# Eight projection tiles of the first block as three products of rounded parts, and the last parameter rows turned earlier

## What is computed

```python
h = rms_norm(x, mix_norm_g[l])
proj = h @ w_in                               # 256 x 1024 by 1024 x (1664 + 512)
qa, ka, va, pb, qm = split_cols(proj, ...)    # attention q, k, v; ten tiles for the recurrence; memory q
pb = token_shift(pb, rwkv_mu[l])              # p + mu * (previous token's p - p)
r, k, v, wd, ad, gd = split_cols(pb, ...)
w = -softplus(-(w0 + tanh(wd) @ w2)) - 0.5    # three low-rank products: w2, a2, g2
a = sigmoid(a0 + ad @ a2)
g = sigmoid(gd) @ g2
kk = k * k_k; kk = kk / norm(kk); k = k * (1 + (a - 1) * k_a)
y = rwkv7_scan(r, w, k, v, -kk, kk * a)       # a recurrence over the tokens
mkv = rms_norm(mem, mem_norm_g) @ w_mem_kv    # keys and values of 256 memory tokens
x = x + concat([out_a, out_b, out_m]) @ w_out
```

## Time and profile before

| | |
|---|---|
| median of 3 runs | 1076.56 us (1076.35 to 1080.98) |
| the profiled execution's own time | 1078.08 us |
| its span, first to last instruction | 1076.3 us |
| PE busy | 915.3 us, 85% of the span |
| DVE busy | 540.1 us, 50% |
| ACT busy | 347.4 us, 32% |
| POOL busy | 76.2 us, 7% |
| mean granted TensorE clock | 0.941 of full |
| read from HBM | 312.24 MB, 291 GB/s over the span |

### The profile page before, as it was taken

How to read it: one execution, slowest core, us unless ns; L and a number is a source line. 1 busy time by engine, 2 the same in 40 slices (tenths; PEclk the granted TensorE clock), 3 DMA queues, 4 the chain that set the end, 5 groups by cost and what they waited for, 6 DMA issues and landing times.

```text
span 1076.3 us, 19223 instructions
## 1 busy us (share of the span) xinstructions
PE 915.3 (85%) x8378; PEld 703.6 (65%) x8378; DVE 540.1 (50%) x1008; ACT 347.4 (32%) x684; POOL 76.2 (7%) x113
## 2 busy tenths in 40 slices
PE   9999999999999999999999997766666666657665
PEld 8587788489999888988989954433333333334432
DVE  2476588858888767888767642211112111212121
ACT  4411355246776526455553331000001000000001
POOL 3101810000000000330010000000000000000000
PEclk9999999999999999999999999988889787889888
DMA  9344463685454664975446999999999999999994
GB/s 347 108 172 170 147 236 101 223 287 173 157 185 160 221 233 162 289 244 189 160 150 253 428 382 421 429 427 430 429 429 427 429 427 431 428 429 431 426 430 173
DMA packets 76106, 316.71 MB, mean 294 GB/s; under 512 B 3999, under 2 KB 27840, under 8 KB 63472
## 3 DMA queue, kind: packets, MB, share of 16 engines
q1 hardware_dynamic: 71252, 302.24, 71.3%
q0 software_dynamic: 4624, 13.14, 4.0%
q10 hardware_dynamic: 140, 0.04, 0.0%
HBM read 312.24 MB, written 1.06 MB: 291 GB/s over the span
## 4 chain that ended last, share of the span: by engine, by line
PE 59%; DMA 27%; DVE 8%; ACT 4%; issue 2%; ACTq 0%; SPq 0%; POOL 0%; DVEq 0%
PE ps L461 57%; DMA w<-in_w_up 19%; DMA w<-in_w_gate 6%; DMA w<-in_w_down 2%; DVE sp L1860 1%; DMA rot<-q 1%; PE ps L587 0%; PE ps L2702 0%; DVE acc L923 0%; ACT sp L1851 0%; ACT hts L2809 0%; ACT sd L2183 0%; PE ps L2115 0%; ACTq L3041 0%; DVE w L961 0%
## 5 line engine op out<-in xcount | busy, mean ns | idle before, releaser
L461 PE MATMUL ps<-w,xg 128*32 128x256 f32 x2048 | 158.9, 474 | 107.4 <-DMA w<-in_w_up 83.8
L461 PE MATMUL ps<-hb,sp 128*128 128x256 f32 x1824 | 224.5, 283 | 0.0
L461 PEld LDWEIGHTS ps<-hb,sp 128*128 128x128 f32 x1824 | 218.6, 188 | 3.9 <-issue 3.0
L461 PEld LDWEIGHTS ps<-w,xg 128*32 128x32 f32 x2048 | 84.4, 132 | 180.3 <-issue 156.3
L1860 DVE TENSOR_TENSOR sp<-w,sp 128x1024 fp32r<-128x1024 f32 x122 | 144.4, 1220 | 37.1 <-ACT sp L1851 37.1
L1851 ACT ACTIVATE sp<-w 128x1024 fp32r<-128x1024 f32 x122 | 122.1, 1051 | 42.1 <-PE ps L461 40.5
L2876 DVE TENSOR_TENSOR cst<-ps,cst 64x256 f32<-64x256 f32 x31 | 13.3, 428 | 224.0 <-ACT cst L2796 224.0
L2796 ACT ACTIVATE cst<-ps 64x256 f32<-64x256 f32 x31 | 11.7, 377 | 324.9 <-PE ps L461 324.9
L2902 DVE TENSOR_TENSOR ost<-ps,cst 32x256 f32<-32x256 f32 x120 | 50.5, 420 | 100.2 <-PE ps L461 97.4
L461 PE MATMUL ps<-w,hts 128*32 128x256 f32 x1024 | 62.1, 382 | 13.2 <-ACT hts L2809 11.4
L461 PE MATMUL ps<-sp,ab 128*128 128x512 f32 x264 | 61.7, 395 | 0.0
(11 more groups left out here) (415 smaller groups left out, 1164.4 us busy)
## 6 DMA issues: line engine op xcount, KB each, us to landing
w<-in_w_down SPq DMA_DIRECT2D x36, 2048.0 KB, 35.1
w<-in_w_gate SPq DMA_DIRECT2D x32, 2048.0 KB, 28.6
w<-in_w_up SPq DMA_DIRECT2D x32, 2048.0 KB, 32.4
w<-in_w_in SPq DMA_DIRECT2D x13, 2048.0 KB, 9.6
w<-in_w_up SPq DMA_DIRECT2D x22, 1024.0 KB, 7.7
w<-in_w_ada SPq DMA_DIRECT2D x8, 2048.0 KB, 8.5
w<-in_w_out SPq DMA_DIRECT2D x4, 2048.0 KB, 9.0
w<-in_w_ada POOLq DMA_DIRECT2D x8, 768.0 KB, 5.3
```

The costliest lines, as they stand in the source:

```text
L461: return q.eng.matmul(o, l, r, start=start, stop=stop, skip_group_check=True)
```

## The change

Eight of the tiles (9, 4, 5, 6, both tiles of the memory queries, 0 and 1) are done by `split_pe` in three float32r products for each k; tiles 8, 3, 2 and 7 and all others stay float32. For them ACT makes the high part of the input in four pieces (`h_hi_sc`) and of each tile's weights (`w_hi_sc`), DVE the low parts (`h_lo_ve`, `w_lo_ve`); the weights' low parts are written over the weights in their slot. `split_pe` waits until a tile's low part is there. The new buffers lie where other things lay, so some of those have moved (`va`, `vm`, `kb`) and two of POOL's DMAs wait: the spread bias for the memory queries, the gate biases for the fourth pair. The last two turns of parameter rows now stand after the first group of low-rank products, the bias product after the second. DVE and ACT do their work in another order. Two semaphores are merged with others, and the counts of the parts go up by 12; nothing else changes.

```diff
--- before.py
+++ after.py
...
@@ -186,9 +186,9 @@
         swb = sb("swb", P1 + 3216, 1536)
         swr = sb("swr", P1 + 4752, 1536)
         qk = sb("qk", P1 + 6288, 2048)
-        va = sb("va", P1 + 8336, 256)
-        vm = sb("vm", P1 + 8592, 512)
-        kb = sb("kb", P1 + 9104, 256)
+        va = sb("va", P1 + 9104, 256)
+        vm = sb("vm", P1 + 8336, 512)
+        kb = sb("kb", P1 + 8848, 256)
         cat = sb("cat", 41264, 2048)
         P_ = [sb(f"pr{i}", o, 512) for i, o in enumerate((44592, 45216, 45728))]
         PT_ = [sb(f"pt{i}", 46240 + 512 * i, 512) for i in range(2)]
@@ -209,6 +209,9 @@
         rs = sb("rs", 44592, 512)
         hT1 = sb("ht1", 45216, 2048)
         mT = sb("mt", 47264, 2048)
+        hT_hi, hT_lo = sb("hth", 27808, 2048, R), sb("htl", P1 + 6800, 2048, R)
+        slotr = [sb(f"wr{i}", 4096 * i, 4096, R) for i in range(3)]
+        w_hi = [sb(f"wh{i}", o, 1024, R) for i, o in enumerate((P1 + 3216, P1 + 4240, P1 + 5264, 41264, 49312, 43568))]
         rqs, rqt, nsink, vmu, yss = (RK[:, o:o + n] for o, n in ((0, 20), (20, 20), (40, 6), (48, 12), (64, 24)))
 
         pz = sb("pz", RB, 2570)
...
@@ -621,6 +625,58 @@
         def proj_pe(q, o, w, c0, act_v, ks=range(8)):
             for k in ks:
                 t = mm(q, o, w[:, k, c0:c0 + 128], act_v[:, k, :], k == 0, k == 7)
+            return t
+
+        SPLIT = [9, 4, 5, 6, ("q", 0), ("q", 1), 0, 1]
+        W_HI = {9: 0, 4: 1, 5: 3, 6: 2, ("q", 0): 1, ("q", 1): 5, 0: 4, 1: 0}
+        HI_AT = {w: 5 + n for n, w in enumerate(SPLIT)}
+
+        def w_of(w):
+            if w in R_AT:
+                c, c0 = R_AT[w]
+                return chunks["in", c], c0
+            return chunks["in", 0], 256 + 128 * w[1]
+
+        def whole(ch, c0, r=False):
+            return (slotr if r else slot)[ch.slot_no].rearrange("p (k n) -> p k n", k=8)[:, :, c0:c0 + 128]
+
+        def w_hi_sc(q, w):
+            ch, c0 = w_of(w)
+            q.wait_ge(*ch.tok)
+            if w in (9, ("q", 0), ("q", 1)):
+                q.wait_ge(s["in_a"], 16)
+            if w == ("q", 0):
+                q.wait_ge(s["rp"], 2)
+            if w == 1:
+                q.wait_ge(s["rp"], 1)
+            if w == 0:
+                q.wait_ge(s["nsc"], 6)
+            q.eng.activation(v(w_hi[W_HI[w]], 8), whole(ch, c0), ACT.Copy).then_inc(s["nhi"], 1)
+
+        def w_lo_ve(q, w):
+            ch, c0 = w_of(w)
+            q.wait_ge(s["nhi"], HI_AT[w])
+            q.eng.tensor_tensor(whole(ch, c0, True), whole(ch, c0), v(w_hi[W_HI[w]], 8).bitcast(F), SUB).then_inc(s["nlo"], 1)
+
+        def piece(a, i):
+            return v(a, 8)[:, 4 * (i % 2):4 * (i % 2) + 4, 128 * (i // 2):128 * (i // 2) + 128]
+
+        def h_hi_sc(q):
+            for i in range(4):
+                q.wait_ge(s["ht1"], i + 1)
+                q.eng.activation(piece(hT_hi, i), piece(hT1, i), ACT.Copy).then_inc(s["nhi"], 1)
+
+        def h_lo_ve(q):
+            for i in range(4):
+                q.wait_ge(s["nhi"], i + 1)
+                q.eng.tensor_tensor(piece(hT_lo, i), piece(hT1, i), piece(hT_hi, i).bitcast(F), SUB).then_inc(s["nlo"], 1)
+
+        def split_pe(q, o, w, ks):
+            ch, c0 = w_of(w)
+            q.wait_ge(s["nlo"], HI_AT[w])
+            hi, lo = v(w_hi[W_HI[w]], 8), whole(ch, c0, True)
+            for k in ks:
+                t = mm3(q, o, [hi[:, k, :], lo[:, k, :]], [v(p, 8)[:, k, :] for p in (hT_hi, hT_lo)], k == 0, k == 7)
             return t
 
         def rpair_steps(q, n):
@@ -631,7 +687,8 @@
                 ch = chunks["in", c]
                 q.wait_ge(*ch.tok)
                 for k in range(0, 8, 2):
-                    t = proj_pe(q, psum[b][:, 256 * h:256 * h + 256], cols8(ch, 128 if c == 4 else 512), c0, hv, (k, k + 1))
+                    o = psum[b][:, 256 * h:256 * h + 256]
+                    t = split_pe(q, o, tile, (k, k + 1)) if tile in SPLIT else proj_pe(q, o, cols8(ch, 128 if c == 4 else 512), c0, hv, (k, k + 1))
                     if h == 1 and k == 6:
                         t.then_inc(s["rp"], 1)
                         free[b] = [(s["rp_sb"], n + 1)]
@@ -640,11 +697,11 @@
         def first_pair_pe(q):
             take(q, 0)
             w = cols8(chunks["in", 0], 512)
-            for h, tile in enumerate(PAIRS[0]):
-                for z in range(2):
-                    q.wait_ge(*((s["in_a"], 16), chunks["in", 0].tok)[z])
-                    q.wait_ge(s["ht1"], 3 + z)
-                    t = proj_pe(q, psum[0][:, 256 * h:256 * h + 256], w, R_AT[tile][1], hv, range(4 * z, 4 * z + 4))
+            for z in range(2):
+                q.wait_ge(*((s["in_a"], 16), chunks["in", 0].tok)[z])
+                q.wait_ge(s["ht1"], 3 + z)
+                proj_pe(q, psum[0][:, 0:256], w, R_AT[8][1], hv, range(4 * z, 4 * z + 4))
+            t = split_pe(q, psum[0][:, 256:512], 9, range(8))
             t.then_inc(s["rp"], 1)
             free[0] = [(s["rp_sb"], 1)]
 
@@ -689,7 +746,8 @@
             w = cols8(chunks[name], 512)
             for z in range(4):
                 h = z // 2
-                t = proj_pe(q, psum[b][:, 256 * h:256 * h + 256], w, c0 + 128 * h, mv_ if n == 3 else hv, range(4 * (z % 2), 4 * (z % 2) + 4))
+                o, ks = psum[b][:, 256 * h:256 * h + 256], range(4 * (z % 2), 4 * (z % 2) + 4)
+                t = split_pe(q, o, ("q", h), ks) if n == 0 else proj_pe(q, o, w, c0 + 128 * h, mv_ if n == 3 else hv, ks)
                 if z == 3:
                     t.then_inc(s["qp"], 1)
                     free[b] = [(s["qk_sb"], 3 * n + 3)]
@@ -771,6 +829,7 @@
             q.wait_ge(s["bias_v"], 1)
             e.dma_start(scratch.ap(), Eb[0:6, :]).then_inc(s["bias"], 16)
             q.wait_ge(s["bias"], 16)
+            q.wait_ge(s["qp"], 1)
             e.dma_start(v(swr, 6), bass.AP(scratch, 0, [[1, 128], [384, 6], [1, 256]])).then_inc(s["bias"], 16)
 
         BANDB = (7, 1, 7)
...
@@ -3043,15 +3102,24 @@
             e.activation(sml(111, 1), cpad[:, 0:1], ACT.Sqrt)
             norms_sc(q, 0, x, (s["x_io"], 16), junk1)
             roots_sc(q, 0)
+            h_hi_sc(q)
+            w_hi_sc(q, 9)
             rpair_sc(q, 0)
+            w_hi_sc(q, 4)
+            w_hi_sc(q, 5)
             cpad_sc(q)
             lt_sc(q)
             norms_sc(q, 1, v(Xm, 2), (s["mem"], 16), junk1)
             rpair_sc(q, 1)
+            w_hi_sc(q, 6)
             lora_sc(q, 0)
+            w_hi_sc(q, ("q", 0))
             lora_sc(q, 1)
             rpair_sc(q, 2)
+            w_hi_sc(q, ("q", 1))
             lora_sc(q, 2)
+            w_hi_sc(q, 0)
+            w_hi_sc(q, 1)
             exp_sc(q)
             lam_sc(q)
             qpair_sc(q, 0)
@@ -3110,18 +3178,27 @@
             scaled_ve(q, 0, x, Xn)
             q.wait_ge(s["par_v"], 1)
             feat_ve(q, 0, hT1, col("mix_norm_g", 0, 8), "ht1")
+            h_lo_ve(q)
+            w_lo_ve(q, 9)
             par_ve(q, 1, 7)
             shift_ve(q, 0)
+            w_lo_ve(q, 4)
+            w_lo_ve(q, 5)
             norms_ve(q, 1)
             shift_ve(q, 1)
+            w_lo_ve(q, 6)
             scan_ve(q)
-            lam1_ve(q)
+            w_lo_ve(q, ("q", 0))
             par_ve(q, 2, 5)
             par_ve(q, 3, 6)
+            shift_ve(q, 2)
+            w_lo_ve(q, ("q", 1))
+            lam1_ve(q)
+            kksq_ve(q)
+            w_lo_ve(q, 0)
             bias_ve(q)
-            shift_ve(q, 2)
-            kksq_ve(q)
             kp_ve(q)
+            w_lo_ve(q, 1)
             hsum_ve(q, 0, HSB, rs, 1.0, 0.0, floor=1e-24)
             scaled_ve(q, 1, v(Xm, 2), Xm)
             feat_ve(q, 1, mT, col("mem_norm_g", 0, 8), "ht1")
@@ -3192,6 +3269,7 @@
             for d, src in plist2:
                 e.dma_start(d, src).then_inc(s["par2"], 16)
             bias_gp(q)
+            q.wait_ge(s["rp"], 4)
             e.dma_start(gb[0], bc(A["b_ada_2"][:, 2048:3072], [128, 1024])).then_inc(s["gb"], 16)
             for j in range(4):
                 e.dma_start(gq[32 * j:32 * j + 32, :], bc(A["b_ada_2"][:, 5120 + 256 * j:5376 + 256 * j], [32, 256])).then_inc(s["gb"], 16)
@@ -3239,11 +3317,13 @@
             for z in range(3):
                 for _ in lora_pe(q, z):
                     next(dense, END)
-            q.wait_ge(s["par2"], N_PAR2)
-            par_pe(q, 2, 5)
-            par_pe(q, 3, 6)
-            q.wait_ge(s["cst2"], 32)
-            bias_pe(q)
+                if z == 0:
+                    q.wait_ge(s["par2"], N_PAR2)
+                    par_pe(q, 2, 5)
+                    par_pe(q, 3, 6)
+                if z == 1:
+                    q.wait_ge(s["cst2"], 32)
+                    bias_pe(q)
             for _ in dense:
                 pass
             hsum_pe(q, 0, HSB, [bsv[:, i, :] for i in range(3)], "hs", (s["r_kk"], 2))
...
```

(5 more changed lines are left out.)

16 lines of the change are left out of this document (8 added, 8 removed).

## The result

The changed kernel takes **1083.06 us** (median of 21 executions, 1077.50 to 1095.61); the kernel before, run beside it, 1080.38 (21 executions, 1076.35 to 1083.83). The ratio is **1.0029, 95% interval 1.0016 to 1.0042**: 2.7 us slower by the medians, less than the 0.5% that the prediction took as what a measurement can tell, but more than this one is uncertain. The ratio is not the quotient of the two medians (1.0025): it is formed from the fast executions alone, without that of 1095.61, which shows a slower state. Forecast were 1076.0, in 1072.8 to 1079.0, and 0.6 us *less* than before. Of the 7.1 us between 1076.0 and 1083.06, 3.8 lie in the starting point: the forecast began from a median of three executions, 1076.56, and 21 have their median at 1080.38. The other 3.3 are the sign: 2.7 more in place of 0.6 less.

What follows compares the result with a forecast made beforehand. PE's work and holes were taken to bound the first 80 us, early gains or losses lasting to the end. Saved 9.5 less paid 8.9 leaves 0.6 us: 1076.56 - 0.6 = 1076.0, range 1072.8 to 1079.0.

Steps and rivals of the forecast that it cites:

- What PE saves: PE's split tiles: three float32r products take 0.351 us against 0.437 for one float32; 64 products save 5.5 us.
- Tile 9: After tile 8, PE waits 0.75 us for tile 9's low part, ready at 16.95 us.
- Tile 6: After three low-rank products, PE waits 0.9 us for tile 6's low part, ready at 32.4 us.
- The turned rows: At 34.9 us PE wants bank 5 and waits 1.4 us for DVE's copy of the first turn.
- The hole at the sums: After the queries, at 48.1 us, PE waits 0.6 us until the bias is out of bank 7.
- The new hole: Before the memory's transposes PE waits 3.3 us for the scaled memory; the clock drops, other holes leave it up.
- The sum: Ledger up to the end of tile 1: saved 9.5 us, paid 8.9 in holes and slow transposes, 0.6 left.
- the first rival: More is kept: ACT and DVE quicker or the clock stays; gain 2.3 up to 5.7 us; 22%.
- Slower, by the clock: Holes of 0.9 and 1.4 us drop the clock there, 1.75 us more per place; 1077.7 to 1079.5; 15%.
- From there the order is that of before: After tile 1, pair (2, 7) is float32 in both and ACT's and DVE's work follows PE; 0.6 us kept.
- It does not reach the end: The attention and recurrence stage may take up what comes sooner at 63 us; then 1076.5; 10%.
- Edits at nothing: POOL's delayed spread bias and gate biases, moved buffers, merged semaphores and SP's queue cost nothing.

Runs made afterwards that it cites:

- e5: Changed kernel with 37 one-column products for 7 warm-ups (8502 products); 1081.92 us, ratio 1.0023.
- e9: Changed kernel with five small DVE writes in front of the parameter copies, to lengthen PE's wait in bank 5; 1086.11 us, ratio 1.0077.
- e2: Kernel before with 39 one-column products for 7 of 12 warm-ups, so 64 more products; 1080.73 us, ratio 1.0018.
- e4: Changed kernel's order with all products float32 and no high or low parts; 1078.03 us, ratio 0.9990.
- e6: Changed kernel with DVE's two parameter-row copies moved before the first query tile's low part; 1079.18 us, ratio 1.0010.
- e7: e6 with two short products in front of the waits for tiles 9 and 6, four warm-ups fewer; 1078.07 us, ratio 0.9985.
- e8: e7 with the memory's transposes after tile 1 as well; 1075.61 us, ratio 0.9963.
- e10: e8 with warm-up and filling products joined to half as many of 256 columns (8418 products); 1073.76 us, ratio 0.9953.
- e11: e10 with parts for tiles 9, 4, 5 and 6 only (8386 products); 1075.02 us, ratio 0.9957.
- e3: Changed kernel with the memory's transposes one tile later, after tile 1; 1079.1 us, ratio 0.9998.
- e12: Changed kernel a third time, no edit; 1084.56 us, ratio 1.0026 to the kernel before.
- e1: Changed kernel again, no edit; 1082.17 us, ratio 1.0019 to the kernel before.

## Why the prediction was wrong, point by point

**What held.** "What PE saves": 0.12 per float32r product. "Tile 9", "Tiles 4 and 5", "Tile 6", "The turned rows", "To the last low-rank product" and "The hole at the sums" gave 0.75, 0, 0.9, 1.4 and 0.6 us of waits in the right places; measured 0.35, 0, 0.50, 0.99 and 0.18. Each is 0.4 too long, in the main because DVE and ACT were ready a little sooner than listed (tile 9's low part at 16.64, not 16.95; two high parts in 2.00, not 2.1). The 0.2 for chunk 1 did not come: tile 3 starts at 19.78. "The new hole": 3.3 forecast, 3.29 measured. "The sum": a lead of 0.6 at `rq_pe`, 1.26 measured. For an execution like the first profile, in which the clock stays up before 52 us and falls behind the new hole, this part is right. One sum in the rivals is off: the gain with all of the first rival is 0.6 + 1.75 + 3.65 = 6.0, not 5.7.

**The step that failed: the clock behind the small waits.** The step "The new hole" says: "the other four are 1.4 or less, and a hole of 1.29 us within 540 to 546 left the clock at 1.00". From that one row, in a dense stream, I took it that such waits are safe, and the ledger has nothing for the clock behind them. In two of the three profiles of the changed kernel the clock fell at 36 to 38 us, just behind the wait of 1.03; so it did in e5, which has the same waits. e9 made that wait longer, and the clock fell there too. Of eight profiles without the wait in bank 5 (before, e2, e4, e6, e7, e8, e10, e11) none has a fall between 12 and 49 us; e3 has the wait and no fall. So a wait of 1.0 us there brings the fall in some executions and not in others, 3 of 5. The prediction's own sign of being wrong, "several windows at 0.50 before 50 us", is what these profiles show.

That the wait brings the fall rests on this count of profiles. The times fit it, but do not prove it. e6 takes away that wait alone and its median is 2.7 us lower than that of e5 on the same chip; e7 takes away the other two as well and is 1.1 lower again. e3 and e8, which ran on two chips, differ in the three waits and in what took them away: `rq_pe` is 1.0 us sooner in e8, and the ratio is lower by 0.0035, which is 3.8 us. The intervals of each pair overlap, and e9's median is no further above e12's than its longer wait explains. No kernel has the wait of 1.0 without the two small ones in front of it, so their share stays open. Taken together, waits, hole and instructions are shown to hold the loss: e10, with less of all three, is 10.8 us under the changed kernel beside it (e12), and the eighth evacuation of `xz` comes 10.9 sooner in its profile (147.21 beside 158.12). What decides in one execution whether the clock falls was not found either.

**The clock behind the large hole.** "The hole before was 2.2 and dropped the clock, so this one will too" is not a rule either. e2 has the hole of 2.21 and e7 that of 3.29, and in both the clock stays up behind it; in before, the changed kernel's first profile, e6, e9 and e12 it falls. And e1, e2 and e11 have a fall 2 to 3 us after `rq_pe` begins, with PE busy, though e11 has no wait before its fall. So the 1.8 us saved and the 1.75 us paid for slow clock in "The sum" belong to two single executions; a fall can be there or not.

**The size of it.** The rival "Slower, by the clock" names this mechanism and this place, with 15%. Its price was wrong too: 1.75 us for each place, "as long as the slow stretch of before", 3.5 us. The slow stretches measured were 10 and 17 us long, and `rq_pe` came 4.2 to 4.8 later. "Slower than 1081.9" was given 5% and "three places of slow clock"; one place is enough. The Trainium skill (TensorE: Matmul & The Clock Gate, Terms) puts the penalty at about the throttled time times the share of pulses that is lost. For e12 that is the sum of what the windows between 36 and 47 us lack, 5.1 us; its sums started 4.8 later than in the first profile, of which 0.3 was there before the fall. The trace agrees within 0.6. In e1 the same rule gives 8.5, and the sums are 7.5 late, 1.0 less. The shorter hole and the full clock behind it give 3.3 of these back by `rq_pe`; the fall at 68 us takes 1.65 again.

**The other step: "From there the order is that of before".** The rival "It does not reach the end" (10%) had the right stage and the wrong reason. The order is the same, but PE's program in front of it is longer, by 64 products and 64 weight loads, and "Edits at nothing" put that at nothing without naming it. Over all profiles:

| products beyond the 8378 of before | kernels | xz 1 to 8, us |
|---|---|---|
| 0 | before, e4 | 22.77, 22.77 |
| 8 | e11 | 22.77 |
| 40 | e10 | 23.31 |
| 64 | changed (3 profiles), e2, e3, e6 to e9 | 24.01 to 24.70 |
| 124 | e5 | 23.98 |

e2 shows that more of PE's instructions, placed ahead, are enough, and e4 that being sooner is not the cause. The price of 64 products is 1.2 to 1.9 us. It doesn't grow in proportion: 8 cost nothing, 40 cost 0.54, and 124 cost 1.2. That it comes from loads of instructions which fall into a stage of many short products is only argued: the idle is called issue, but e5 did not behave as fixed steps would.

**Does an early loss reach the end?** Yes. From the eighth evacuation to the end of the span it is 923.3 us before and between 922.4 and 926.9 in the thirteen others, while that evacuation itself moves from 147.2 to 159.4. The prediction's first sentence on this held. The 4.5 us between 922.4 and 926.9 follow no edit; they are the last stage's own spread, as large as the effects looked for here.

**Put together.** An execution without the early fall has 1.26 less at `rq_pe` and 1.5 more in the recurrence, 0.25 in all: no change. With the fall, the first evacuation of `xz` comes 4.8 (e12) and 5.8 us (e1) later than in the first profile. The falls were seen in two of three profiles. If they come in half of the executions or more, a median some 2 to 5 us above before is an estimate from these figures; measured are 2.7, 2.2 and 5.5 by the medians in the three groups, and 3.1, 2.1 and 2.8 by the ratios. The share of executions with a fall is not measured. Both mistakes were hidden in the two profiled executions compared first: 1077.50 is the fastest of its 21, and 1078.08 lies 2.3 below the median that before had beside it.

## What to carry to other kernels

Fill the gaps of about 1 us that a reordering opens in PE's stream, or move what they wait for: what they cost is not only their length but the half clock that may follow, here 10 to 17 us long in three of five profiles. Don't book such a fall as certain or as absent from one profile: a hole of the same length had one behind it in one profile and none in another. Splitting a product into more instructions has a price outside the place where they stand; count them, and look for waits for issue in a later stage of short products. Don't take the starting point from three executions when they spread by more than the effect; here that was 3.8 us of the miss. And look at the spread: if the profiled execution is the fastest of its kernel, a second profile of the same kernel is the cheapest experiment there is.
